# Issuing engine of the three squared-block stores in a Strassen-like feed-forward: from SyncE's queue to ScalarE's

## The chip, the core and the metric

The kernel runs on one core of a Trainium2 chip. The metric is the device time of one execution in microseconds, lower is better. A core has TensorE (matmuls), VectorE, ScalarE, GpSimd and SyncE, which only waits and issues DMAs. Each engine works through its own instructions in order; between engines there are semaphores only. ScalarE can issue DMAs too: its queue hands instructions to the engine and issues the DMAs that stand between them.

## The reference, cut to what matters

Two layers of a streaming encoder for 1024 prompt tokens and 8 x 16 sample tokens (1152 together), width 1024: a mixer (attention with a convolution in layer 0, an mLSTM in layer 1), and after each mixer a feed-forward with hidden width 4096:

```python
def sq_relu_ffn(x, g, w1, w2):
    h = jax.nn.relu(rmsnorm(x, g) @ w1)
    return (h * h) @ w2
...
xp = xp + sq_relu_ffn(xp, norm_ffn_g[l], w_ff1[l], w_ff2[l])
xs = xs + sq_relu_ffn(xs, norm_ffn_g[l], w_ff1[l], w_ff2[l])
```

Everything is float32.

## The kernel before, in words

Channels lie on the 128 partitions, tokens in the free dimension. A float32 product is made from three passes: weights and activations are split into a high and a low part, and high x high, high x low and low x high are summed in PSUM.

The feed-forward (function `ffn` of each engine's program, called with f = 0 and f = 1 for the two layers) uses a Strassen-Winograd scheme: a 2 x 2 block product is made from seven products instead of eight. Tokens are halved (h = 0, 1; 576 tokens each), and so are the channels. The up-projection runs over 16 **pairs** p of hidden tiles (`PAIRS`), each of them seven products of 24 matmuls of 288 columns. The down-projection then runs over 32 units d. What the down-projection needs of the hidden activations are seven blocks of 128 x 576 per pair: the squared blocks B11, B22 and B21, and the sums T1 to T4. They don't all fit on the chip, so they are stored to DRAM (tensor `ffn_rows`, 288 KB a block) and read back chunk by chunk (`rows_in`, line 588). The squared block B12 (c12) isn't stored as such except in two pairs of the second layer.

One pair, by engine:

- **TensorE** (line 987 in `product`): products 0 to 6 of the pair. Product 2 adds to the PSUM bank that product 0 left, so it waits until ScalarE has copied that bank (`copied`). Products 4 and 6 wait for VectorE's reads (`up_read`).
- **ScalarE**: at the pair's beginning it waits for `t_out` (the blocks' buffers were read by VectorE), `c_out` (the stores of B11 and B22 of the pair before have landed) and `f_done`, then copies product 0's bank into c11 (`copied_out`, line 2332), takes the high part of a weight block (`weights`, line 2260), copies product 1's bank into c22, takes the high parts of six more weight blocks, and between these squares the four blocks in place (`squared`, line 2320, in the order c11, c22, c12, c21; semaphore `h_sq`). The square of c21 is the last instruction of the pair; the next is the copy into c11 of the next pair. In a layer's first pair the squares of c11, c22 and c12 stand directly behind each other, since they wait for the row norm. In its last pair the high parts of the chunk-0 operands (`rows_high`, line 2329) stand between them.
- **VectorE**: adds products (`joined`, line 1596), applies the relu with the norm's factor (`relu`, line 1599), and makes the sums T1 to T4 (`t_sum`, line 1603; semaphore `t_out`). Its first `joined` of a pair waits for `up_out`: the stores of T1, T3, T2 and B21 of the pair before.
- **GpSimd**: the weight sums (line 741) and the low parts of the weights (line 727, semaphore `f_split`).
- **SyncE** (function `feed`): per pair and in this order: wait for the first square and store B11; wait until GpSimd has split the pair's last weights and load the weights of pair p + 2 (line 569); wait for the second square and store B22; store T1, T3 and T2, each behind its `t_out`; wait for the fourth square and store B21; store T4 behind its `t_out`. In the last pair the reads of chunk 0 stand between these.

All these stores are issued on line 577, in `keep`. The semaphores that count their landing are `c_out` (B11, B22), `up_out` (T1, T2, T3, B21) and `t4_out` (T4).

Of the kernel before, what the change touches and what calls it, by code (L numbers as in the profile page):

```python
# [82 lines left out]
HELD = ("B11", "B21", "B22", "T1", "T2", "T3", "T4")  # L83
# [79 lines left out]
def build(nc, t):  # L163
    es = ExitStack()
    with es:
# [382 lines left out]
        @block.sync  # L548
        def _(sp):
            def load(u, s, split):  # L550
                if split is not None:
                    sp.wait_ge(w_split, split)
                if u < U_OUT0:
                    row = IN_ORDER[u]
                elif u < U_GATE:
                    row = U_OUT0 + OUTS[u - U_OUT0]
                elif u < U_OUT1:
                    row = W_GATE + u - U_GATE
                else:
                    row = W_GATE + U_OUT1 - U_GATE + OUTS[u - U_OUT1]  # L560
                sp.dma_start(w_raw[:, s, :], t["wall"][row]).then_inc(w_in[s], 16)

            def feed(f, units):
                base, n0 = W_FF[f], NP * f

                def up_load(p):
                    c, i = divmod(p, 2)
                    for o in range(2):
                        sp.dma_start((w_raw, w_more)[p % 2][:, o, :], t["wall"][base + 8 * c + i + 2 * o])\
                            .then_inc(w_in[p % 2], 16)  # L570

                def down_load(d):
                    c, j = divmod(d, 4)
                    sp.dma_start(w_raw[:, d % 2, :], t["wall"][base + 8 * c + 4 + j]).then_inc(w_in[d % 2], 16)

                def keep(p, o):
                    sp.dma_start(ffn_rows[p // 2, HELD.index(o), :, p % 2, :], kept[o])\
                        .then_inc({"B11": c_out, "B22": c_out, "T4": t4_out}.get(o, up_out), 16)

                def rows_in(c, i):  # L580
                    n = staging(c, i)[0]
                    o = OPERAND[DOWN[i]]
                    if o == "T4":
                        sp.wait_ge(t4_out, 16 * (PAIRS * f + 2 * c + 2))
                    else:
                        sp.wait_ge(c_out, 32 * (PAIRS * f + 2 * c + 2))
                        sp.wait_ge(up_out, 64 * (PAIRS * f + 2 * c + 2))
                    sp.dma_start(stage_at[n], ffn_rows[c, HELD.index(o)]).then_inc(staged[n], 16)

                def next_rows(c, i):  # L590

                    q = 7 * (c - 1) + i
                    if q == 0:
                        sp.wait_ge(c_relu, 4 * PAIRS * (f + 1))
                    else:
                        sp.wait_ge(d_lo, 14 * FC * f + 14 + 2 * (q - 1))
                    rows_in(c, i)

                sp.wait_ge(w_split, units)
                up_load(0)  # L600
                sp.wait_ge(ssq_done, KT * (2 * f + 2))
                up_load(1)
                for p in range(PAIRS):
                    n = PAIRS * f + p
                    if p == PAIRS - 1:
                        sp.wait_ge(d_lo, 14 * FC * f + 2)
                        rows_in(0, 1)
                        sp.wait_ge(f_split, n0 + NPU)
                        rows_in(0, 2)
                        sp.wait_ge(f_done, n0 + NPU - 7 + 3)  # L610
                        rows_in(0, 3)
                        rows_in(0, 4)
                    sp.wait_ge(h_sq, 4 * n + 1)
                    keep(p, "B11")
                    if p < PAIRS - 1:
                        sp.wait_ge(f_split, n0 + 7 * (p + 1))
                        if p + 2 < PAIRS:
                            up_load(p + 2)
                        else:
                            sp.wait_ge(w_in[1], 16 * (rows_before(f, 1) + PAIRS))  # L620
                            down_load(0)
                            down_load(1)
                            rows_in(0, 0)
                    else:
                        sp.wait_ge(d_lo, 14 * FC * f + 4)
                        rows_in(0, 5)
                    sp.wait_ge(h_sq, 4 * n + 2)
                    keep(p, "B22")
                    if p == PAIRS - 1:
                        sp.wait_ge(d_lo, 14 * FC * f + 6)  # L630
                        rows_in(0, 6)
                    if f == 1 and p >= PAIRS - 2:
                        sp.wait_ge(h_sq, 4 * n + 3)
                        sp.dma_start(ffn_b12[:, p % 2, :], c12).then_inc(b12_out, 16)
                    sp.wait_ge(t_out, 4 * n + 1)
                    keep(p, "T1")
                    sp.wait_ge(t_out, 4 * n + 2)
                    keep(p, "T3")
                    sp.wait_ge(t_out, 4 * n + 3)
                    keep(p, "T2")  # L640
                    sp.wait_ge(h_sq, 4 * n + 4)
                    keep(p, "B21")
                    sp.wait_ge(t_out, 4 * n + 4)
                    keep(p, "T4")
                next_rows(1, 0)
                sp.wait_ge(c_out, 32 * PAIRS * (f + 1))
                sp.wait_ge(up_out, 64 * PAIRS * (f + 1))
                sp.wait_ge(t4_out, 16 * PAIRS * (f + 1))
                for k in range(4):
                    if k == 1 and f == 1:  # L650
                        sp.wait_ge(b12_out, 32)
                    if k == 3:
                        sp.wait_ge(d_lo, 14 * FC * f + 12)
                    sp.dma_start(x[:, 4 + k, :], x_hold[k]).then_inc(x_in[4 + k], 16)
                for d in range(DUNITS):
                    c, j = divmod(d, 4)
                    if c + 1 < FC:
                        for i in range(max(2 * j, d == 0), min(2 * j + 2, 7)):
                            next_rows(c + 1, i)
                    elif f == 1 and j == 0:  # L660
                        sp.wait_ge(d_lo, 14 * FC * (f + 1))
                        sp.wait_ge(b12_out, 32)
                        sp.dma_start(stage_at["rbc"], ffn_b12).then_inc(staged["rbc"], 16)
                    if d + 2 < DUNITS:
                        sp.wait_ge(f_split, n0 + NPU + 7 * (d + 1))
                        down_load(d + 2)

            load(0, 0, None)
            load(1, 1, None)
            load(2, 0, 1)  # L670
            load(3, 1, 2)

            sp.wait_ge(taps_turned, 1)
            for g in range(NG):
                sp.dma_start(taps_dram[:, :, g, :], taps_rev[GC * g:GC * (g + 1), :, :]).then_inc(taps_out, 16)
            sp.wait_ge(taps_out, 16 * NG)
            sp.wait_ge(pads, 1)
            for f in range(PH):
                sp.dma_start(shifted[f::PH, :, f:f + CW], taps_dram.rearrange("c j g r -> c (j g) r"))\
                    .then_inc(taps_in, 16)  # L680
            for u in range(4, U_OUT0):
                load(u, u % 2, u - 1)
            for u in range(U_OUT0, U_GATE):
                load(u, u % 2, u - 1)
            feed(0, U_GATE)
            sp.wait_ge(f_split, NP - 7)
            load(U_GATE, 0, None)
            sp.wait_ge(f_split, NP)
            load(U_HEAD, 1, None)
            for u in range(U_HEAD + 1, N_UNITS):  # L690
                load(u, u % 2, u - 1)
            feed(1, N_UNITS)
            for i in range(NL):
                for k in range(KT - POOL_Y):
                    sp.wait_ge(y_done, (KT - POOL_Y) * i + k + 1)
                    sp.dma_start(t["y"][k][:, qtok(i)], x[:, k, qtok(i)]).then_inc(y_out, 16)
                for k in range(POOL_Y if i < NL - 1 else 0):
                    sp.wait_ge(y_pool, POOL_Y * i + k + 1)
                    sp.dma_start(t["y"][KT - POOL_Y + k][:, qtok(i)], x[:, KT - POOL_Y + k, qtok(i)])\
                        .then_inc(y_out, 16)  # L700
# [1509 lines left out]
        def _(act):  # L2210
# [19 lines left out]
            def ffn(f, b_out):  # L2230
# [86 lines left out]
                def squared(p, n):  # L2317
                    act.wait_ge(c_relu, 4 * (p0 + p) + n + 1)
                    c = (c11, c22, c12, c21)[n]
                    A(c, c, ACT.Square).then_inc(h_sq, 1)  # L2320

                def rows_high(c, i):
                    n, per, count = staging(c, i)
# [678 lines left out]
```

## Time and profile before

| | |
|---|---|
| median of 3 runs | 2778.97 us (2775.98 to 2780.82) |
| profiled execution | 2784.48 us, its span 2782.7 us |
| granted TensorE clock, mean | 0.978 |
| TensorE busy (matmul) | 2624.5 us, 94% |
| VectorE busy | 1727.5 us, 62% |
| ScalarE busy | 953.3 us, 34% |
| GpSimd busy | 1492.9 us, 54% |
| DMA | 308.21 MB, mean 111 GB/s |

The up-projection lies at about 480 to 870 us in the first layer and at about 1990 to 2380 us in the second. Busy shares tell where the work is, not what bounds it; for that one reads what the idle time of TensorE waited for, and then the timeline of the engine that released it.

### The profile page before, as it was taken

What the parts mean: (1) busy time and instruction counts of PE and PEld (TensorE: products, weight loads), DVE (VectorE), ACT (ScalarE), POOL (GpSimd) and SP (SyncE); (2) the same over time, 40 slices, a digit from 0 to 9 for tenths busy, and PEclk for the clock granted to TensorE, in tenths of its full rate; (3) what the DMA queues carried; (4) which work ended last, traced back from release to release, by engine and by line L of the source; (5) the groups of instructions that cost most, each with busy time, mean ns of one, the idle gap of its engine ahead of it and who ended that gap; (6) DMA issues with size and microseconds to landing.
All of it is one profiled execution on the core that took longest, in us unless ns stands there. A gap on an engine that the chain in (4) does not pass through costs nothing. (4 is left out here: it accounts for less than half of the span.)

```text
span 2782.7 us, 44112 instructions
## 1 busy us (share of the span) xinstructions
PE 2624.5 (94%) x17357; PEld 2533.1 (91%) x17357; DVE 1727.5 (62%) x2295; ACT 953.3 (34%) x1824; POOL 1492.9 (54%) x1527
## 2 busy tenths in 40 slices
PE   7999998999997999999999999989889999799998
PEld 7997698899997999999999898979889999699997
DVE  5217946666666777778646464654756666677776
ACT  3113734333333444442413223232433333344444
POOL 6543423566665878773222222252366665588783
PEclk9999989999999999999999999999999999899999
DMA  6321031333335444432232242433133334544432
GB/s 194 71 54 33 4 116 55 113 131 128 133 129 199 147 139 140 140 122 81 43 107 32 93 58 73 82 116 116 57 141 131 130 130 156 185 140 148 140 131 92
DMA packets 161789, 308.21 MB, mean 111 GB/s; under 512 B 61628, under 2 KB 76988, under 8 KB 160816
## 3 DMA queue, kind: packets, MB, share of 16 engines
q1 hardware_dynamic: 86656, 243.19, 25.9%
q10 hardware_dynamic: 74656, 61.22, 7.5%
q8 instruction: 139, 2.28, 0.4%
q0 software_dynamic: 272, 0.98, 0.1%
q14 instruction: 66, 0.54, 0.1%
HBM read 204.18 MB, written 95.85 MB: 108 GB/s over the span
## 5 line engine op out<-in xcount | busy, mean ns | idle before, releaser
L727 POOL TENSOR_TENSOR w_lo<-w_raw,w_hi 128x256 fp32r<-128x256 f32 (+1 forms) x478 | 433.9, 920 | 280.9 <-ACT w_hi L2260 280.7
L987 PE MATMUL psum<-a_hi,w_hi 128*128 128x288 f32 x2032 | 438.5, 298 | 13.2 <-DVE low L1703 10.8
L987 PE MATMUL psum<-op_h,w_hi 128*128 128x288 f32 x2040 | 369.8, 305 | 79.1 <-ACT low L2332 38.1
L1703 DVE TENSOR_TENSOR low<-low,psum 128x576 f32<-128x576 f32 x441 | 330.4, 750 | 172.3 <-PE psum L987 170.0
L987 PE MATMUL psum<-a_lo,w_hi 128*128 128x288 f32 x2032 | 437.2, 297 | 0.0
L987 PE MATMUL psum<-a_hi,w_lo 128*128 128x288 f32 x2032 | 437.0, 297 | 0.0
L2260 ACT ACTIVATE w_hi<-w_raw 128x256 fp32r<-128x256 f32 (+1 forms) x478 | 209.8, 456 | 565.7 <-POOL w_raw L741 366.6
L987 PEld LDWEIGHTS psum<-op_h,w_hi 128*128 128x128 f32 x2040 | 310.4, 195 | 88.4 <-issue 64.6
L987 PEld LDWEIGHTS psum<-a_hi,w_hi 128*128 128x128 f32 x2032 | 330.3, 190 | 14.7 <-DVE low L1703 11.7
L987 PEld LDWEIGHTS psum<-a_lo,w_hi 128*128 128x128 f32 x2032 | 329.8, 190 | 0.0
L987 PEld LDWEIGHTS psum<-a_hi,w_lo 128*128 128x128 f32 x2032 | 329.6, 190 | 0.0
L932 PE MATMUL psum<-a_hi,w_hi 128*128 128x384 f32 x1272 | 302.8, 346 | 17.5 <-DVE a_lo L1511 16.0
L714 POOL TENSOR_SCALAR w_hi<-w_raw 128x1024 fp32r<-128x1024 f32 x63 | 71.2, 1131 | 429.5 <-issue 364.7
L932 PE MATMUL psum<-a_lo,w_hi 128*128 128x384 f32 x1272 | 291.5, 337 | 0.0
L932 PE MATMUL psum<-a_hi,w_lo 128*128 128x384 f32 x1272 | 290.9, 336 | 0.0
L932 PEld LDWEIGHTS psum<-a_hi,w_hi 128*128 128x128 f32 x1272 | 225.1, 189 | 25.0 <-issue 13.8
L741 POOL TENSOR_TENSOR w_raw<-w_raw 128x256 f32<-128x256 f32 (+1 forms) x237 | 232.3, 980 | 16.5
L1596 DVE TENSOR_TENSOR low<-low,psum 128x576 f32<-128x576 f32 x128 | 96.5, 754 | 221.0 <-PE psum L987 221.0
L932 PEld LDWEIGHTS psum<-a_hi,w_lo 128*128 128x128 f32 x1272 | 228.8, 189 | 0.0
L932 PEld LDWEIGHTS psum<-a_lo,w_hi 128*128 128x128 f32 x1272 | 228.3, 189 | 0.0
L987 PE MATMUL psum<-op_h,w_lo 128*128 128x288 f32 x1020 | 224.4, 302 | 0.0
L1603 DVE TENSOR_TENSOR low<-low 128x576 f32<-128x576 f32 x128 | 173.7, 1375 | 60.0 <-ACT low L2320 57.0
(313 smaller groups left out, 4617.0 us busy)
## 6 DMA issues: line engine op xcount, KB each, us to landing
w_raw<-in_wall SPq DMA_DIRECT2D x159, 512.0 KB, 4.5
ffn_rows<-low SPq DMA_DIRECT2D x224, 288.0 KB, 2.1
mid<-ffn_rows SPq DMA_DIRECT2D x52, 576.0 KB, 3.7
rbc<-ffn_rows SPq DMA_DIRECT2D x50, 576.0 KB, 3.7
mid<-in_wall SPq DMA_DIRECT2D x32, 512.0 KB, 4.4
low<-in_x ACTq DMA_DIRECT2D x16, 576.0 KB, 8.8
high<-in_mem_in ACTq DMA_DIRECT2D x32, 257.0 KB, 4.2
out_mem_s<-high ACTq DMA_DIRECT2D x32, 257.0 KB, 3.2
```

Source lines behind the costliest of these rows:

```text
L714: nc.gpsimd.tensor_scalar(w_hi[:, s, :], w_raw[:, s, :], 1.0, 1.0, ALU.mult, ALU.mult)\
L727: nc.gpsimd.tensor_tensor(w_lo_flat[:, at], src, w_hi_flat[:, at].bitcast(F32), ALU.subtract)\
L741: nc.gpsimd.tensor_tensor(dst, one, other, op).then_inc(f_sum, 1)
L932: r = mm(psum[:, z + i, 0:TN], w[:, s, k * P:(k + 1) * P], a[:, kk, tok(i)], start=first and n == 0, stop=last and n == 2)
L987: r = mm(psum[:, bank + i, 0:QT], v[:, at.start + P * k:at.start + P * (k + 1)], rows(part, k)[:, qtok(i)], start=start and k == 0 and n == 0,
L1596: V.tensor_tensor(by2(dst), by2(one), other, ALU.add).then_inc(up_read, 1)
L1603: V.tensor_tensor(dst, one, other, ALU.subtract).then_inc(t_out, 1)
L1703: V.tensor_tensor(dst, dst, two(bank), ALU.add).then_inc(dn_read, 1)
L2260: A(w_hi_flat[:, at], src, ACT.Copy).then_inc(f_high, 1)
```

## The change

The stores of B11, B22 and B21 leave SyncE's program. ScalarE issues them directly behind the square that makes the block: it waits for its own square (`h_sq`) and then issues the DMA on its own queue. Destination, source, size and counting semaphore are the same. The store of B12 and those of T1 to T4 stay on SyncE. There are 3 x 16 x 2 = 96 such stores.

```diff
@@ feed (SyncE) @@
                         rows_in(0, 3)
                         rows_in(0, 4)
-                    sp.wait_ge(h_sq, 4 * n + 1)
-                    keep(p, "B11")
                     if p < PAIRS - 1:
                         sp.wait_ge(f_split, n0 + 7 * (p + 1))
                         if p + 2 < PAIRS:
...
                         rows_in(0, 5)
-                    sp.wait_ge(h_sq, 4 * n + 2)
-                    keep(p, "B22")
                     if p == PAIRS - 1:
...
                     keep(p, "T2")
-                    sp.wait_ge(h_sq, 4 * n + 4)
-                    keep(p, "B21")
                     sp.wait_ge(t_out, 4 * n + 4)
                     keep(p, "T4")
@@ squared (ScalarE) @@
                     c = (c11, c22, c12, c21)[n]
                     A(c, c, ACT.Square).then_inc(h_sq, 1)
+                    if n != 2:
+                        o = ("B11", "B22", None, "B21")[n]
+                        act.wait_ge(h_sq, 4 * (p0 + p) + n + 1)
+                        dma(ffn_rows[p // 2, HELD.index(o), :, p % 2, :], c).then_inc(up_out if n == 3 else c_out, 16)
```

## Rows read from the trace of the kernel before

**Rows 1.** Waits of TensorE: engine, line, waited for: us in total, times, longest.
```profile
PE psum L987 <- ACT low L2332: 38.1, 30, 5.3
```
**Rows 2.** Timeline of TensorE: start, us, what, in brackets idle before and releaser.
```profile
587.85 0.76 PE L987 MATMUL psum<-op_h,w_hi 128*128 128x288 f32 x4 [0.84 <-ACT low L2332]
```
**Rows 3.** Timeline of ScalarE over a regular pair.
```profile
573.70 0.69 ACT L2320 ACTIVATE low<-low 128x576 f32<-128x576 f32 x1 [2.01 <-DVE low L1599]
576.27 0.63 ACT L2260 ACTIVATE w_hi<-w_raw 128x512 fp32r<-128x512 f32 x1 [1.89 <-POOL w_raw L741]
576.83 0.69 ACT L2320 ACTIVATE low<-low 128x576 f32<-128x576 f32 x1
579.61 0.63 ACT L2260 ACTIVATE w_hi<-w_raw 128x512 fp32r<-128x512 f32 x1 [2.10 <-POOL w_raw L741]
...
586.48 0.68 ACT L2320 ACTIVATE low<-low 128x576 f32<-128x576 f32 x1 [5.11 <-DVE low L1599]
587.07 0.63 ACT L2332 ACTIVATE low<-psum 128x576 f32<-128x576 f32 x1
```
**Rows 4.** Chain that ended last, second layer, around a pair's beginning: start, us, what.
```profile
2283.99 0.02 ACTq L2254
2284.01 0.07 issue
...
2284.46 0.64 ACT low L2332
...
2285.24 22.63 PE psum L987 x168
```
**Rows 5.** Timeline of SyncE's queue, same pair.
```profile
574.77 0.43 SPq L569 DMA_DIRECT2D mid<-in_wall  x1
...
587.19 0.32 SPq L577 DMA_DIRECT2D ffn_rows<-low  x1
```
**Rows 6.** Timeline of GpSimd, same pair: the last weights of pair p.
```profile
568.56 1.29 POOL L727 TENSOR_TENSOR w_lo<-mid,w_hi 128x512 fp32r<-128x512 f32 x1 [1.15 <-ACT w_hi L2260]
```
**Rows 7.** Timeline of ScalarE and its queue in the convolution part.
```profile
121.80 0.67 ACT L2467 ACTIVATE high<-low 128x256 f32<-128x256 f32 x1
122.50 0.34 ACTq L2470 DMA_DIRECT2D out_conv_p<-high  x1
122.87 0.60 ACTq L2471 DMA_DIRECT2D out_conv_s<-high  x1
123.51 0.38 ACT L2480 ACTIVATE low<-psum 128x256 f32<-128x256 f32 x1 [1.04 <-issue]
```
**Rows 8.** Issues: ns min/median/max, first and last start; then KB and median us to landing.
```profile
L2285 ACTq DMA_DIRECT2D x_hold<-low x8: 326/330/333, 389.7 to 1981.3; - x8
L577 SPq DMA_DIRECT2D ffn_rows<-low x224: 319/320/1052, 506.0 to 2395.1; - x112
...
ffn_rows<-low SPq DMA_DIRECT2D x224, 288.0 KB, 2.1
mid<-ffn_rows SPq DMA_DIRECT2D x52, 576.0 KB, 3.7
```
**Rows 9.** Timeline of VectorE, the same pair's first sum of products.
```profile
591.40 0.76 DVE L1596 TENSOR_TENSOR low<-low,psum 128x576 f32<-128x576 f32 x1 [3.45 <-PE psum L987]
```
**Rows 10.** Timeline of ScalarE, from the first layer's first pair to its second.
```profile
505.27 2.03 ACT L2320 ACTIVATE low<-low 128x576 f32<-128x576 f32 x3 [0.83 <-DVE low L1599]
...
512.28 0.68 ACT L2320 ACTIVATE low<-low 128x576 f32<-128x576 f32 x1 [4.46 <-DVE low L1599]
513.66 0.65 ACT L2332 ACTIVATE low<-psum 128x576 f32<-128x576 f32 x1 [0.69 <-DMA ffn_rows<-low]
```
**Rows 11.** Timeline of ScalarE in the first layer's last pair.
```profile
858.63 0.67 ACT L2320 ACTIVATE low<-low 128x576 f32<-128x576 f32 x1
863.35 1.17 ACT L2329 ACTIVATE a_hi<-mid 128x1152 fp32r<-128x1152 f32 x1 [4.04 <-DMA mid<-ffn_rows]
```
**Rows 12.** Timeline of SyncE's queue there.
```profile
859.57 0.32 SPq L588 DMA_DIRECT2D mid<-ffn_rows  x1
```

## The prediction

> **What bounds the kernel now.** I read the waits first. TensorE's own idle time in the up-projection names one releaser: 30 waits, 38.1 us, for the PSUM copy of line 2332 on ScalarE [rows 1]. There are 30 pairs with a predecessor (15 in each of two layers), so it is one wait per pair. The size of one stands at the matmul behind it: 0.84 us idle [rows 2]. So this short wait lies on the path that sets the end, once per pair, and whatever delays that copy delays everything.
>
> Then I read ScalarE's timeline over one pair of about 23.45 us [rows 3]. The square of c21 starts at 586.48, as soon as VectorE's relu lets it. The copy of the next pair's first product starts at 587.07, 0.59 us later, which is before the square's recorded end (586.48 + 0.68 = 587.16): the two overlap in the engine. The copy reads the pair's first product, and TensorE has done a second one since; so PSUM isn't what it waits for, it stands behind the square in ScalarE's order. TensorE goes on 0.15 us after the copy. The chain in the second layer has the same copy (0.64 us) [rows 4].
>
> The other two squares that will get a store have slack behind them: the next instructions, at 576.27 and 579.61, had idled 1.89 and 2.10 us for GpSimd's weights [rows 3].
>
> **What the change does, part by part.**
>
> Removed from SyncE: 96 issues (3 per pair, 32 pairs) of 0.32 us and the waits for the squares. SyncE computes nothing, so the issue time is worth nothing. What stood behind the waits is the question. The load of a pair's weights two pairs ahead was issued at 574.77, directly behind c11's square (573.70 + 0.69) and its 0.32 us issue [rows 3, 5]. GpSimd had split the last weights of the overwritten buffer at 568.56 + 1.29 = 569.85 [rows 6]. The load will thus go out about 4.9 us earlier. Nobody waits for it: in ScalarE's order its first reader (line 2357 of the next pair) stands almost a pair's time behind it, and even a transfer of 576 KB lands in 3.7 us [rows 8]. Value 0. The stores of T1, T3, T2 and T4 wait for their own sums, as before.
>
> Added to ScalarE: 3 own waits and 3 issues per pair. What one costs shows in the convolution part, which has the same pattern, an operation, a wait for it, two issues, an operation on PSUM [rows 7]. The operation ends at 121.80 + 0.67 = 122.47, the issue begins at 122.50 (0.03), the last one ends at 122.87 + 0.60 = 123.47, and the next operation starts at 123.51 (0.04). Nothing overlaps any more. An issue of a tile of 128 rows takes 0.33 us on ScalarE's queue and 0.32 us for these very stores on SyncE's [rows 8].
>
> Behind c21's square the cost is whole. The copy now starts 0.68 (square) + 0.03 + 0.33 + 0.04 after the square's start. The separate semaphore instruction ahead of the copy, which now runs under the square, comes behind the issue: such an instruction takes 0.02 + 0.07 = 0.09 us [rows 4]. That makes 1.17 us in place of 0.59, **0.58 us more**. The loop closes through TensorE: a later copy makes later products, relus and squares, while TensorE's work between (22.63 us, 168 matmuls [rows 4]) stays. So 28 regular pairs give 28 x 0.58 = 16.2 us.
>
> Behind c11's and c22's squares one costs 0.03 + 0.33 + 0.04 plus the lost overlap of 0.1, some 0.5 us, against 1.89 and 2.10 us of idle time. Value 0. If GpSimd became faster, that cover would go and each would cost 0.5.
>
> The stores themselves land as before. c21's was issued at 587.19 [rows 5] and goes out at 586.48 + 0.68 + 0.03 = 587.19 now. VectorE needs its buffer free at 591.40 [rows 9]; a store of this size lands in 2.1 us [rows 8], at 589.3. Margin 2.1 us.
>
> The first pair of a layer has its squares back to back (three in 2.03 us, 0.67 apart) with no slack [rows 10]. With two issues between them they stand 0.68 + 0.03 + 0.33 + 0.04 = 1.08 apart: the third is 0.8 us late, then the last square (512.28) too, and the copy comes at 512.28 + 0.8 + 1.17 = 514.25. It was at 513.66, not at 512.87, since it waited 0.79 us for the c22 store, which stood behind the weight load on SyncE's queue. That wait goes. Net 0.6 us, twice: 1.2 us.
>
> The last pair of a layer: c11's square (858.63) is followed by a copy that idled until 863.35 for a load [rows 11]; the issue hides there. The store goes out at 859.33, however, and the load that is waited for at 859.57 [rows 12], where before the store came behind it. Sizes 288 and 576 KB land in 2.1 and 3.7 us [rows 8], so 288 KB keep the engines busy for some 1.6 us. Shared fully, the load is at most 1.6 - 0.24 = 1.3 us later; with transfers side by side it is near nothing. I take 0.3 us, twice: 0.6 us. c22's and c21's issues there delay operand copies that are read later.
>
> Also on the time of these two issues: SyncE begins one at 859.57 while ScalarE's runs (859.33 to 859.66). The Trainium skill (Perfetto Trace Analysis, "DMA Instruction — HWDGE") says that the descriptor generator is shared by the sequencers that issue and locked for exclusive use, so that one issue waits for the other. By it, 0.1 us would be added twice and the sum would be 0.2 us longer.
>
> **Sum:** 16.2 + 1.2 + 0.6 = 18.0 us. The profiled execution took 2784.48 us (span 2782.7), 5.5 us above the median of 2778.97. It would become 2802.5; the median becomes 2797.0, 0.65% slower.
>
> **Bounds.** The cost per pair: below, without the 0.09 and with 0.32, 0.48 us, 14.4 us for 30. Above, the slowest issue of these stores on SyncE, 1.05 us [rows 8], gives 1.30 us per pair; it happens where the queue is full, and at c21's place it isn't, so I go up to 0.75 us as usual size: 22.5 us. Layer ends: from a gain of 1 us in all (loads out sooner) to 2.6 us. That gives 13.4 to 25.1 us, and the runs scatter by 3 us below and 2 above: 2789 to 2806.
>
> **Rivals.**
>
> *The issue hides.* ScalarE's queue hands the store over and the copy starts under it; only the lost overlap and the own wait remain, 0.12 us x 30 = 3.6 us, 2782.6 us. For it: an issue runs in ScalarE's queue and not in the engine, as its own rows show, so it could go on beside the engine's work. Against it: with an own wait, rows 7 show the next operation only after the issue. Chance 0.07.
>
> *Not slower: SyncE's order was the brake.* The c22 store no longer stands behind a 1 MB load in the first pair (0.79 us, twice), and loads and row reads at the layer ends leave earlier by an issue and its gap, 0.4 us twice. That is 2.4 us gained, and it decides only if a pair costs less than 0.08 us. With no cost at all: 2776.6 us. Little speaks for it, as TensorE's waits name ScalarE and not a transfer. Chance 0.04, nearly all of it within 0.2%.
>
> *The issue costs far more than 0.33 us.* The rule on the locked generator would do this where both queues issue at once. In a regular pair SyncE's T4 store goes out 0.8 us after c21's place, so the two miss each other by 0.46 us; if each c21 issue nevertheless took the 1.05 us of the slowest row, 30 x 1.30 + 1.8 = 40.8 us, 2820 us. The Trainium skill's page, just named, is the reason to keep this case. The trace shows no such row in regular pairs. Chance 0.09.
>
> *The issues behind c11 and c22 also reach the path.* From the point where a square, its issue and the split exceed 1.89 us of slack, 30 x 0.5 us more: 2812 us. Chance 0.03.
>
> That the change doesn't do what it says I give nothing: the three stores are issued either way.
>
> **How the numbers follow.** The forecast has 0.77: 2797.0 us. The range 2787 to 2808 holds its bounds and some more on both sides; the other cases lie outside. A measurement of this kernel can tell about 0.2% (5.6 us) from no change. Slower: 0.77 + 0.09 + 0.03 = 0.89, and a little of the first rival, so 0.89. The same: 0.09. Faster: 0.02.
>
> **What would show it.** TensorE's wait for line 2332 grows from 38.1 to about 55 us in 30 waits (0.84 to 1.42 us in a regular pair). ScalarE's queue shows 96 issues of about 0.33 us, each 0.03 us behind its square. The copy stands 1.17 us behind c21's square. Idle time behind the other two squares stays, smaller by the issue. The weight loads start near 569.9 in place of 574.8, relative to the pair. The copy in the first pairs names no transfer any more. It would be wrong if the copy started before the issue's end, or if the pair's period stayed at 23.45 us.

## The result, and the profile after

The changed kernel takes 2810.76 us (median of 4 runs, 2807.82 to 2812.96) against 2779.89 us before (2775.98 to 2781.32). The ratio is 1.0113, with a 95% interval of 1.0095 to 1.013: 31 us slower, where I had forecast 18 us slower and at most 2808 us. The direction was right, the size was too small by 13 us. The profiled executions, 2784.48 us before and 2807.82 us after, lie 23.3 us apart.

The wait that the prediction rested on is the same one, and it grew. From the waits of the changed kernel (engine, line, waited for: us in total, times, longest):

```profile
PE psum L981 <- ACT low L2330: 61.3, 30, 5.8
```

It was 38.1 us in 30 waits [rows 1], and about 55 was forecast; the lines have moved, 2330 is the copy of line 2332 and 981 the matmul of 987. ScalarE's timeline over a regular pair, which answers to [rows 3]:

```profile
594.97 0.69 ACT L2314 ACTIVATE low<-low 128x576 f32<-128x576 f32 x1 [2.01 <-DVE low L1593]
595.69 0.33 ACTq L2318 DMA_DIRECT2D ffn_rows<-low  x1
597.55 0.63 ACT L2254 ACTIVATE w_hi<-mid 128x512 fp32r<-128x512 f32 x1 [1.89 <-POOL mid L735]
598.10 0.69 ACT L2314 ACTIVATE low<-low 128x576 f32<-128x576 f32 x1
598.82 0.33 ACTq L2318 DMA_DIRECT2D ffn_rows<-low  x1
600.89 0.63 ACT L2254 ACTIVATE w_hi<-mid 128x512 fp32r<-128x512 f32 x1 [2.10 <-POOL mid L735]
...
607.75 0.68 ACT L2314 ACTIVATE low<-low 128x576 f32<-128x576 f32 x1 [5.09 <-DVE low L1593]
608.46 0.33 ACTq L2318 DMA_DIRECT2D ffn_rows<-low  x1
608.91 0.65 ACT L2330 ACTIVATE low<-psum 128x576 f32<-128x576 f32 x1 [0.48 <-ACT low L2314]
```

The copy starts 1.16 us behind the square (607.75 to 608.91); 1.17 was forecast, 0.59 it had been. The idle time behind the other two squares is unchanged, 1.89 and 2.10 us (it is counted from the engine's last instruction, and the issue runs within it). TensorE's matmul behind the copy, which answers to [rows 2], idled 1.42 us in place of 0.84:

```profile
609.70 0.78 PE L981 MATMUL psum<-op_h,w_hi 128*128 128x288 f32 x4 [1.42 <-ACT low L2330]
```

The weight loads left at 591.15, 6.27 us into their pair, in place of 11.15, which is the forecast 4.9 us earlier. So in a regular pair every step came out. From the start of one such copy to the next the trace has 24.03 us, before 23.45: 0.58 us more. But not every pair is regular any more. Some take 24.4 or 24.66 us and four take 25.5 us or more, which the kernel before did not have at all. In one of the four, TensorE's timeline behind the copy:

```profile
706.24 0.76 PE L981 MATMUL psum<-op_h,w_hi 128*128 128x288 f32 x4 [2.32 <-ACT low L2330]
706.84 0.65 PE L981 MATMUL psum<-op_h,w_lo 128*128 128x288 f32 x2
707.28 1.16 PE L981 MATMUL psum<-op_h,w_hi 128*128 128x288 f32 x4
708.24 0.68 PE L981 MATMUL psum<-op_h,w_lo 128*128 128x288 f32 x2
708.72 1.16 PE L981 MATMUL psum<-op_h,w_hi 128*128 128x288 f32 x4
```

and the stretches there (columns: stretch, length, busy us and count of PE, PEld, DVE, ACT, POOL, then the granted clock, DMA share, GB/s):

```profile
706.90:710.20 3.30, 3.30 (x16) 3.30 (x15) 0.00 (x0) 0.77 (x2) 2.32 (x2) 0.50 0.17 62
710.40:728.00 17.60, 17.60 (x134) 17.60 (x134) 12.20 (x10) 4.96 (x8) 12.39 (x9) 1.00 0.30 111
```

The granted clock is at 0.50 for 3.3 us: the lower level, 1.2 GHz. Ahead of it TensorE had idled 2.32 us, not 1.42. In this profile such an idle time stands behind pairs of 24.4 us, and one of 2.03 us behind pairs of 24.66 us.

What makes those? VectorE and GpSimd change places. In a regular pair VectorE's third relu and GpSimd's third weight sum start within some 10 ns of each other. Timelines of VectorE and GpSimd in a regular pair:

```profile
599.52 1.89 DVE L1593 SCALAR_TENSOR_TENSOR low<-low,rbc 128x576 f32<-128x576 f32 x1
```

```profile
599.51 1.29 POOL L735 TENSOR_TENSOR mid<-mid 128x512 f32<-128x512 f32 x1
```

and the same two in a pair of 24.40 us:

```profile
574.82 0.81 DVE L1593 SCALAR_TENSOR_TENSOR low<-low,rbc 128x576 f32<-128x576 f32 x1
```

```profile
574.98 1.80 POOL L735 TENSOR_TENSOR w_raw<-w_raw 128x512 f32<-128x512 f32 x1
```

and in a pair of 24.66 us:

```profile
2244.78 0.76 DVE L1593 SCALAR_TENSOR_TENSOR low<-low,rbc 128x576 f32<-128x576 f32 x1
```

```profile
2244.78 1.90 POOL L735 TENSOR_TENSOR w_raw<-w_raw 128x512 f32<-128x512 f32 x1
```

One of the two takes its short time and the other waits it out: 1.29 and 1.89 us, or 1.80 and 0.81, or 1.90 and 0.76. In the pairs of 24.66 us it is a tie: the recorded starts lie within 10 ns, over all profiles in either order, and only the durations tell who was first. In the pairs of 24.40 us GpSimd is 156 ns behind: the 168 matmuls took 22.08 us there in place of 22.61, and VectorE's inputs were there sooner (for these two rates see the last section). When GpSimd is second, ScalarE's weight block comes 0.5 to 0.6 us later, behind it in ScalarE's order the square of c12, then VectorE's three sums and the square of c21. TensorE's next idle time is 2.03 us after the tie, and 2.32 us after the pair of 24.40 us, in which TensorE had also finished sooner. I call both kinds ties below. The Trainium skill (SBUF — State Buffer, "Who interferes with whom") has the rule: the two share a port pair that is locked for a whole instruction, and the order of issue decides who blocks. The trace agrees on the blocking, with the six durations above; the order within 10 ns its records can't show. The rule was there to be read, and the kernel before has such pairs too (four of the 26, 24.06 us), but I hadn't seen that TensorE's next idle time grows with them.

Counted for every profile of this study, over pairs 3 to 15 of each layer (26 pairs; ties are pairs with the relu under 1 us, falls are pairs in which the granted clock goes to 0.50), with the median of each kernel's runs (the kernels ran on several chips, on which the one before took 2776.4 to 2779.9 us):

| kernel | regular pair, us | ties | falls | median, us |
|---|---|---|---|---|
| before | 23.45 | 4 | 0 | 2779.9 |
| changed | 24.03 | 11 | 4 | 2810.8 |
| changed, again | 24.04 | 7 | 3 | 2810.9 |
| only c21's store | 24.04 | 10 | 5 | 2809.7 |
| only c11's and c22's stores | 23.45 | 4 | 0 | 2778.0 |
| one wait, no issue | 23.60 | 9 | 0 | 2785.4 |
| nine waits, no issue | 24.04 | 2 | 1 | 2797.3 |
| nine waits, again | 24.04 | 5 | 2 | 2802.6 |
| changed, idle time filled | 23.98 | 10 | 0 | 2797.5 |
| before, idle time filled | 23.50 | 0 | 0 | 2775.4 |
| c21's store behind the copies | 23.45 | 7 | 0 | 2782.3 |
| copy first, before | 22.40 | 11 | 0 | 2747.4 |
| copy first, changed | 22.40 and 21.84 | 11 | 0 | 2735.7 |

With the copy first, a tie costs nothing: in the second layer of that kernel without the change, pairs take 22.40 us with a relu of 0.76 us as in the first layer with one of 1.90 us.

### The profile page after: what moved, and what is told of

Same layout as the page of the kernel before. It is cut to its first block and busy times, and to the rows that moved or that the text cites. A ratio compares the mean times of both kernels' runs of the same rounds, so it can differ in the third digit from the quotient of the medians.

```text
span 2806.0 us, 44112 instructions
## 1 busy us (share of the span) xinstructions
PE 2620.6 (93%) x17357; PEld 2530.7 (90%) x17357; DVE 1722.4 (61%) x2295; ACT 956.4 (34%) x1824; POOL 1497.3 (53%) x1527
```

## The experiments

My theory after the result: the issue of c21's store ahead of the copy costs 0.58 us a pair (serial), and the longer idle time brings TensorE to half clock (clock). The rival: stores on a second queue and weight loads that start earlier disturb transfers (transfer). The kernels of the first four runs shared one chip; the kernel before took 2776.36 us there.

**Only c21's store moved.**

```diff
-                    sp.wait_ge(h_sq, 4 * n + 4)
-                    keep(p, "B21")
...
+                    if n == 3:
+                        act.wait_ge(h_sq, 4 * (p0 + p) + n + 1)
+                        dma(ffn_rows[...]).then_inc(up_out, 16)
```

> Only c21's store is issued by ScalarE; those of c11 and c22 stay on SyncE. Serial theory (the issue stands ahead of the copy of line 2332, and only there does it cost): the regular pair is 24.03 us as in the changed kernel, in place of 23.45, and the whole time is within 4 us of the changed kernel (2807 to 2813). Transfer theory (stores on a second queue and earlier loads disturb each other): only a part of the 31 us, 2785 to 2800.

Measured: 2809.65 us, ratio 1.0126 (1.0111 to 1.0141), regular pair 24.04 us. One third of the moved stores makes the whole cost.

**Only c11's and c22's stores moved.** The condition is `if n < 2`, and SyncE keeps c21's.

> Only the stores of c11 and c22 are issued by ScalarE; c21's stays on SyncE. Serial theory: regular pair 23.45 us, whole time within 3 us of before (2777 to 2783), if anything faster by the 0.8 us that the first pair's copy waited for a transfer, twice. Transfer theory: 10 to 25 us above before, since two thirds of the moved stores and the earlier weight loads are here.

Measured: 2777.97 us, ratio 1.0007 (0.9998 to 1.0017), regular pair 23.45 us. These two stores cost nothing, and the weight loads, which leave earlier with them, disturb nobody. Transfer theory is out for two of the three moved stores. The first two pairs of each layer together take 56.3 and 57.6 us in place of 57.1 and 58.1. The size would fit the transfer that is no longer waited for (0.8 each), but it shows nothing: the next kernel, in which no store moved, has 56.9 and 56.6.

**The wait without the issue.**

```diff
                     A(c, c, ACT.Square).then_inc(h_sq, 1)
+                    if n == 3:
+                        act.wait_ge(h_sq, 4 * (p0 + p) + 4)
```

> All stores on SyncE; ScalarE only waits for its own square of c21 and issues nothing. It separates the wait from the issue. Serial theory: the square and the copy no longer overlap, 0.12 to 0.25 us per pair in place of 0.58, so 4 to 8 us over before (2783 to 2788), and no clock fall in the regular pairs. If the wait itself were the cost, 17 us or more.

Measured: 2785.38 us, ratio 1.0035 (1.0022 to 1.0048), 9 us above before where 4 to 8 were expected. From ScalarE's timeline:

```profile
655.76 0.68 ACT L2320 ACTIVATE low<-low 128x576 f32<-128x576 f32 x1 [5.09 <-DVE low L1599]
656.48 0.65 ACT L2334 ACTIVATE low<-psum 128x576 f32<-128x576 f32 x1
```

The copy stands 0.72 us behind the square, 0.13 more than before; the pair grew by 0.15. The other 0.43 of the 0.58 is the issue (0.33) and the queue's steps around it. Nine ties in place of four would make some 3 us of the 9. No fall: a tie alone isn't enough where a regular pair idles little; TensorE's idle time behind one is 1.58 us here.

**The changed kernel again.**

> The changed kernel once more, for a second profile. Clock theory (beyond 0.58 us per pair, the excess over my sum is TensorE at half clock in some pairs whose idle time has grown to 2.3 to 2.6 us, and pairs in which VectorE's third relu starts ahead of GpSimd's sum): 2808 to 2813 us, again with three or more regular pairs of 25.5 us or longer, and their number tells the runs apart. If the pairs are clean, the excess lies elsewhere.

Measured: 2810.92 us, ratio 1.0133 (1.0116 to 1.015). Seven ties and three falls in this profile, whose own time of 2801.8 us was the lowest of its runs. Between pairs that are otherwise alike a tie costs 24.66 - 24.04 = 0.6 us and a fall 25.55 - 24.04 = 1.5 us.

The next four shared a chip again; the kernel before took 2779.23 us.

**The idle time filled.** Five small matmuls on constants stand ahead of TensorE's wait for the copy; their result isn't used.

```diff
+                    for i in range(FILL if p > 1 else 0):
+                        mm(psum[:, Z, 384:512], ones, ident, start=True, stop=True, skip_group_check=True)
                     pe.wait_ge(copied, 2 * (PAIRS * f + p) + 1)
```

> The changed kernel, with five small matmuls on constants (their result isn't used) put on TensorE where it idles between the second and third product of a pair. They fill most of the idle time and give nothing back to the path. Clock theory: no half-clock stretch in the regular pairs any more, pairs of 24.03 us and of 24.65 us where VectorE's third relu comes ahead of GpSimd's sum, none of 25.5; the whole time falls from 2811 to 2796 to 2803 us. If the excess over 18 us isn't the clock, it stays at 2808 to 2813.

Measured: 2797.47 us, ratio 1.0058 (1.0039 to 1.0076), no fall, ten ties. TensorE's timeline at the place:

```profile
608.92 1.28 PE L1023 MATMUL psum<-mats 128*128 128x128 f32 x10
611.02 0.79 PE L982 MATMUL psum<-op_h,w_hi 128*128 128x288 f32 x4 [0.82 <-ACT low L2333]
```

This stands behind a tie; behind a regular pair 0.2 us of idle time are left. Work that nobody needs makes the kernel 13 us faster, and no pair falls to half clock any more. Not all of the 13 us is seen in the profiles: pairs 3 to 15 of both layers are together 6.5 us shorter than in the first profile of the changed kernel and 4.0 shorter than in the second. About 1.6 us of it is not the clock: the matmul behind the copy starts 0.70 us after the copy's start in place of 0.79, so that a regular pair takes 23.98 us.

**The same in the kernel before, as a control.**

> The same five matmuls in the kernel before, as a control: its regular pairs had no half-clock stretch, so nothing is to be gained, and the matmuls end inside the idle time. 2774 to 2780 us, regular pair 23.45 us. If they delay the third product, it shows here.

Measured: 2775.43 us, ratio 0.9984 (0.9975 to 0.9993), regular pair 23.50 us. So the filling is worth 3.8 us here as well, perhaps through ties (none in this profile, but each pair is 0.05 us longer). Of the 13.3 us in the changed kernel some 9.5 are its own. With the idle time filled in both, the change costs 2797.47 - 2775.43 = 22.0 us.

**Nine waits, no issue**, all stores on SyncE:

```diff
+                    if n == 3:
+                        for _ in range(9):
+                            act.wait_ge(h_sq, 4 * (p0 + p) + 4)
```

> All stores on SyncE; ScalarE waits nine times for its own square of c21, which is there after the first. A delay without any transfer or issue. A wait of its own costs 0.15 us as measured; each further semaphore instruction 0.09 us, and if two waits share one instruction some 0.4 us in all. Serial theory: the time depends on the delay alone, so a pair that is 0.55 us longer gives the 31 us of the change with its clock falls, 2800 to 2812 us. Transfer theory: 17 us at most, without clock falls.

Measured: 2797.34 us, ratio 1.0062 (1.0044 to 1.008). By chance the delay is exactly that of the change:

```profile
582.05 0.68 ACT L2320 ACTIVATE low<-low 128x576 f32<-128x576 f32 x1 [5.11 <-DVE low L1599]
583.21 0.65 ACT L2335 ACTIVATE low<-psum 128x576 f32<-128x576 f32 x1 [0.47 <-ACT low L2320]
```

1.16 us from square to copy, pair 24.04 us, and no transfer was touched. That gives 18 us of the 31, and already one fall. It is below the 2800 that the serial theory had, with two ties only.

**c21's store behind the copies.** ScalarE issues it behind the second PSUM copy of the next pair:

```diff
                     copied_out(p, c22, V_)
+                    if p:
+                        store_c21(p - 1)
                     weights(n + 1)
```

> As the change, but ScalarE issues c21's store behind the two PSUM copies of the next pair instead of ahead of them. Serial theory: the wait is long over by then, and the issue stands ahead of a weight split with slack; regular pair 23.45 us, no clock fall, 2774 to 2781 us. If VectorE's wait for this store (its margin was 2 us) becomes the limit, the pair grows by less than 0.5 us: 2780 to 2790.

Measured: 2782.32 us, ratio 1.0006 (0.9996 to 1.0015), regular pair 23.45 us. The time is 1.3 us above the serial theory's and inside the other range, but before was at its upper end on this chip (2779.23), and the pair didn't grow, which decides for the serial theory. ScalarE's timeline:

```profile
562.85 0.68 ACT L2314 ACTIVATE low<-low 128x576 f32<-128x576 f32 x1 [5.12 <-DVE low L1593]
563.44 0.63 ACT L2334 ACTIVATE low<-psum 128x576 f32<-128x576 f32 x1
563.56 0.33 ACTq L2322 DMA_DIRECT2D ffn_rows<-low  x1
563.97 0.62 ACT L2254 ACTIVATE w_hi<-kwm 128x512 fp32r<-128x512 f32 x1
```

The store leaves at 563.56, as soon after the square as in the change (0.03 us), and yet the copy starts at 0.59 us again: it had started before the issue (563.44, 563.56), so the queue had handed it over before it came to the wait. All three stores are on ScalarE here: it is the place of the wait and the issue in the order that costs, not the stores on a second queue as such.

The last three shared a chip; the kernel before took 2779.43 us.

**The copy first.** In the kernel before, the copy of the next pair's first product goes ahead of the square of c21:

```diff
                     else:
                         weights(n + 6)
+                        begin_pair(p + 1)
                     squared(p, 3)
```

(`begin_pair` holds the copy and its waits, which stood at the next pair's beginning.)

> The kernel before, with the copy of the next pair's first product (line 2332) put ahead of the square of c21 in ScalarE's order. If that order is what TensorE waited for, its 0.84 us of idle time per pair goes: regular pair 22.6 us, 28 x 0.84 = 24 us and some of the first pairs' wait, 2748 to 2757 us. If VectorE's chain (relus and sums) is the next limit, the pair stays above 23 us and the time above 2765.

Measured: 2747.38 us, ratio 0.9887 (0.9866 to 0.9908). Pair 22.40 us, which is 168 matmuls without a gap; in pairs 3 to 15 TensorE has no wait for this copy any more (two are left, in the layers' second pairs). VectorE's chain isn't a limit at this pace.

**The copy first in the changed kernel.**

> The same order in the changed kernel, with its three stores on ScalarE. Serial theory: nothing on the path stands behind c21's store any more, so it is within 4 us of the copy-first kernel without the change (2748 to 2760). Transfer theory: the cost of the moved stores remains, 10 us or more over it.

Measured: 2735.66 us, ratio 0.9846 (0.9827 to 0.9865). Neither case: with the copy out of the way the moved stores are a gain of 12 us (19 between the two profiles). The first of it is at each layer's beginning, where the first two pairs are 6.1 and 4.7 us shorter. ScalarE's copy into the second pair, in the copy-first kernel without the change and then with it:

```profile
505.34 2.02 ACT L2320 ACTIVATE low<-low 128x576 f32<-128x576 f32 x3 [0.83 <-DVE low L1599]
...
513.39 0.65 ACT L2332 ACTIVATE low<-psum 128x576 f32<-128x576 f32 x1 [5.50 <-issue]
```

```profile
504.73 0.69 ACT L2314 ACTIVATE low<-low 128x576 f32<-128x576 f32 x1 [0.83 <-DVE low L1593]
505.45 0.33 ACTq L2318 DMA_DIRECT2D ffn_rows<-low  x1
505.82 0.69 ACT L2314 ACTIVATE low<-low 128x576 f32<-128x576 f32 x1 [0.40 <-ACT low L2314]
506.54 0.33 ACTq L2318 DMA_DIRECT2D ffn_rows<-low  x1
...
508.67 0.65 ACT L2330 ACTIVATE low<-psum 128x576 f32<-128x576 f32 x1 [0.54 <-DVE low L1597]
```

8.05 us from square to copy without the change, since the stores stand behind 1 MB of weight loads in SyncE's order: that of c22 was issued at 507.41 and landed 5.9 us later, at 513.3. With the change it is 3.94 us. The rest comes from the matmul rate of the second layer (below).

**Nine waits again.**

> The kernel with nine waits and no moved store once more. Its pair had the same 24.03 us as the changed kernel, but the whole was 13 us below it, with one pair at half clock and few pairs in which VectorE came ahead of GpSimd. If that count is chance, the profile now shows 5 to 10 such pairs, three falls or more and 2802 to 2812 us; if it belongs to the kernel, again 2792 to 2800 us with at most 3 of them.

Measured: 2802.61 us, ratio 1.0096 (1.0072 to 1.012); five ties, two falls. Between the two cases: it is in the time range of chance, with one fall too few, and 23 us above before. The slowest of its four runs took 2810.18 us, as the changed kernel does.

## Why the prediction was right or wrong

**The bound** was right: the copy on ScalarE, once per pair. The copy-first kernel shows it by taking it away.

**The cost per pair** was right: 0.58 us forecast, 0.58 measured, made of 0.15 for the wait and 0.43 for the issue. So was its place, c21's store alone; the two others cost nothing, as forecast. The rival that the issue hides is out, and so is the one with a far dearer issue: all 96 took 326 or 327 ns. It would have given 2820 us, near what came, but through something that doesn't happen. The prediction put the slowest issue of 1.05 us, from which this rival and the upper bound start, down to a full queue. No run shows that: it stood at 2390.44 us, with the DMA engines 5% busy in the 2 us before, and what made it long is open. The rival nearest to the result, issues behind c11 and c22 that reach the path (2812 us), is out by the kernel with only those two stores moved (ratio 1.0007).

**The locked generator.** The rule that the prediction cites would have added 0.1 us where SyncE and ScalarE issue at once. The place, from ScalarE's and SyncE's timelines in a layer's last pair:

```profile
866.41 0.33 ACTq L2318 DMA_DIRECT2D ffn_rows<-low  x1
```

```profile
866.64 0.32 SPq L588 DMA_DIRECT2D mid<-ffn_rows  x1
```

They overlap by 0.10 us and neither is longer than alone; the second layer has the same at 2393.35 and 2393.59. These issues don't show the lock.

**The last pair of a layer**: the read issued at 866.64 was in use at 870.59, 3.95 us, against 863.35 - 859.57 = 3.78 before [rows 11, 12]. I had 0.3 us, it was 0.17 in this layer and 0.04 in the second; with none of the three stores moved the same time is 3.64 to 3.89 us from profile to profile, so it is hardly more than scatter. **The first pairs** (57.3 and 57.5 us for the first two, 57.1 and 58.1 before) vary by more than the 0.6 us forecast, with stretches at half clock in both.

**The step that failed** is "TensorE's work between (22.63 us, 168 matmuls) stays", and with it 28 x 0.58 as the sum. The work doesn't stay when the idle time ahead of it grows: in the pairs with a fall the 168 matmuls took 24.13 us in place of 22.61. I took the path as rigid, looked at each slack for whether it covers the issue, and didn't ask what a longer idle time does to TensorE's clock, nor that VectorE and GpSimd stand in a near tie whose two outcomes differ by 0.6 us. In the profiles the 26 regular pairs grew by 23.9 us: 26 x 0.58 = 15.1; four falls at 1.5, 6.0; the other 2.8 is ties (seven at 0.36, three at 0.62 and one at 0.8 in a fall's pair, less four at 0.61 before). Outside these pairs the two profiles differ by less than 1 us in all, so that 7 to 8 us of the 31 between the medians don't show in these two profiles. In the medians the filled kernel shows the fall's part best: with the clock kept up, the changed kernel is 18.2 us above before (2797.47 against 2779.23), where my sum was 18.0. That agreement is partly luck, as the control gained 3.8 us from the same filling.

The upper bound failed with the same step. It took the cost of a pair to 0.75 us and never the consequences of a longer idle time; 2808 us left out the median of 2810.76 by 3 us.

**Open**: why the kernels with c21's store on ScalarE ahead of the copy have more ties and falls (7 to 11, 3 to 5) than the one with nine waits and the same pair time (2 and 5, 1 and 2). With two and three profiles it may be chance; the start of the relu stands within 11 ns of GpSimd's in most pairs of these kernels, so anything that shifts a start by some nanoseconds could do it. The medians (2809.7 to 2810.9 against 2797.3 and 2802.6) say that it is more than chance in one profile. So a part of 8 to 13 us of the change comes only with the moved store, and through which step is argued and not shown. The granted clock of whole runs points at more falls and doesn't settle it: its mean is 0.978 for the changed kernel (eight runs), 0.979 with only c21's store, 0.980 and 0.979 with nine waits, 0.981 before and 0.982 with the idle time filled. Among the eight runs with nine waits the fastest had 0.982 (2792.90 us) and the slowest 0.977 (2810.18 us). It wasn't tried to keep VectorE and GpSimd apart in time.

## What to carry to other kernels

Ahead of a wait for the own engine and a DMA issue, put whatever other engines wait for: here the same three stores cost 31 us with c21's behind the last square, nothing that could be told (ratio 1.0006) with c21's behind the copies, and gave 12 us once the copy went first, part of it by a matmul rate that nothing here explains. If an instruction stands on the path only because of its engine's order, reorder it before anything is added to that order; that was worth 32 us alone and 44 us with the stores. And when a change lengthens a repeated idle time of TensorE, price also the pairs in which it gets long enough for half clock; to leave them out was an error of 13 us in 31.

## What the runs showed that I had not expected

- TensorE's clock went to the lower level in the middle of a regular stretch after idle times of 2.03 to 2.33 us (0.50 for 3.3 us, 1.5 us lost), and in no pair counted in the table behind a shorter one; the longest of those was 1.74 us. It is no fixed consequence: of the 34 such idle times in the five profiles with a regular pair of 24.03 or 24.04 us, 15 were followed by a fall. Pairs with 2.32 us and no fall stand in the same profile, such as this one:

```profile
585.67 0.76 PE L981 MATMUL psum<-op_h,w_hi 128*128 128x288 f32 x4 [2.32 <-ACT low L2330]
```

- The matmul rate has two values at the same granted clock. Stretches of 200 us in which TensorE never idles, one in each layer of the changed kernel with the copy first:

```profile
600.00:800.00 200.00, 200.00 (x1503) 200.00 (x1502) 131.96 (x107) 71.14 (x116) 139.24 (x99) 1.00 0.37 140
2100.00:2300.00 200.00, 200.00 (x1541) 200.00 (x1540) 125.82 (x109) 72.74 (x120) 146.18 (x102) 1.00 0.38 145
```

  1503 matmuls are 133.1 ns each, 1541 are 129.8 ns; it keeps one rate for the whole layer, and pairs take 22.40 or 21.84 us. Over the 13 pairs of the second layer that is 7 us of this kernel's gain. What sets the rate wasn't tried. In the changed kernel it shows for single pairs (24.40 us), in which the 168 matmuls take 22.08 us and VectorE gets ahead of GpSimd by some 155 ns.
- Filling an idle time of 1.4 us, and of 0.8 us in the kernel before, with unused matmuls gained time in both kernels (13.3 and 3.8 us).
